# Gated recurrence: the span products of levels 32, 16, 8 and 4 cut into 64 keys by 32 queries, one half of the array's columns for each half tile, and their picks in two parts

## What is computed

```
def hgrn2_chunkwise(q, log_f, k, v):
    ...
    b = jnp.cumsum(lfc, axis=2)
    o_inter = jnp.einsum('bhtk,bhkv->bhtv', qc * jnp.exp(b), state)
    diff = b[:, :, :, None, :] - b[:, :, None, :, :]
    decay = jnp.exp(jnp.where(causal, diff, -jnp.inf))
    attn = jnp.einsum('bhtk,bhsk,bhtsk->bhts', qc, kc, decay)
    o_intra = jnp.einsum('bhts,bhsv->bhtv', attn, vc)
    b_last = b[:, :, -1, :]
    k_dec = kc * jnp.exp(b_last[:, :, None, :] - b)
    new_state = jnp.exp(b_last)[..., None] * state + jnp.einsum('bhsk,bhsv->bhkv', k_dec, vc)
    return new_state, o_inter + o_intra
```

## Time and profile before

| | |
|---|---|
| median of 3 runs | 2033.02 us (2029.32 to 2034.14) |
| profiled execution, its time | 2031.16 us |
| its span | 2029.2 us, 27449 instructions |
| TensorE busy | 1973.9 us, 97% |
| VectorE busy | 1352.0 us, 67% |
| ScalarE, GpSimd busy | 824.5 us, 941.1 us |
| level products (L1164) | 640 records, from 113.3 to 586.9 us |

### The profile page before, as it was taken

The page is one execution under the profiler, slowest core; times in us unless marked ns, Lnnn a source line. Parts: engine busy times, 40 slices in busy tenths (PEclk is TensorE's granted clock), DMA queues, the critical chain, the costliest instruction groups (busy, mean ns, idle before and its releaser), DMA issues.

```text
span 2029.2 us, 27449 instructions
## 1 busy us (share of the span) xinstructions
PE 1973.9 (97%) x10053; PEld 1623.2 (80%) x10053; DVE 1352.0 (67%) x1784; ACT 824.5 (41%) x1313; POOL 941.1 (46%) x548
## 2 busy tenths in 40 slices
PE   7999999999999999999999899898999999999997
PEld 6888888888887768878888678776888888888886
DVE  7887777666536754687061487798856656667978
ACT  5444444344411014463200476657323323334443
POOL 1354454422324459753354110855755455445553
PEclk8999999999999999999999899999999999999999
DMA  9223222211122244044110200222423323357344
GB/s 285 75 81 117 73 72 103 84 40 31 42 63 58 68 156 135 11 177 126 42 51 11 84 2 1 73 104 80 139 88 109 114 88 109 103 183 242 104 137 164
DMA packets 179501, 193.98 MB, mean 96 GB/s; under 512 B 9863, under 2 KB 122968, under 8 KB 179418
## 3 DMA queue, kind: packets, MB, share of 16 engines
q1 hardware_dynamic: 172996, 178.53, 27.8%
q10 hardware_dynamic: 6422, 14.37, 2.0%
HBM read 151.71 MB, written 41.16 MB: 95 GB/s over the span
## 4 chain that ended last, share of the span: by engine, by line
PE 80%; DVE 10%; ACT 5%; issue 3%; POOL 1%; ACTq 0%; DVEq 0%; POOLq 0%
PE psum L1003 7%; PE psum L1558 7%; PE psum L1560 7%; PE psum L1559 7%; PE psum L1005 6%; PE psum L1004 6%; PE psum L1164 3%; PE psum L1661 3%; PE psum L1662 3%; PE psum L1663 3%; PE psum L1024 3%; PE psum L1025 3%; PE psum L1023 3%; PE psum L1319 2%; PE psum L1321 2%
## 5 line engine op out<-in xcount | busy, mean ns | idle before, releaser
L795 POOL TENSOR_TENSOR w_hi<-w_raw,ones 128x1024 fp32r<-128x1024 f32 x60 | 149.2, 2487 | 481.8 <-PE psum L1005 357.5
L1003 PE MATMUL psum<-h_hi,w_hi 128*128 128x512 f32 x704 | 284.2, 404 | 0.0
L1005 PE MATMUL psum<-h_hi,w_lo 128*128 128x512 f32 x704 | 274.8, 390 | 0.0
L1004 PE MATMUL psum<-h_lo,w_hi 128*128 128x512 f32 x704 | 274.2, 389 | 0.0
L798 POOL TENSOR_TENSOR w_lo<-w_raw,w_hi 128x1024 fp32r<-128x1024 f32 x60 | 166.7, 2779 | 4.7
L1693 ACT ACTIVATE arena<-psum 128x1024 f32<-128x1024 f32 (+7 forms) x103 | 80.3, 787 | 216.4 <-PE psum L1005 136.0
L1003 PEld LDWEIGHTS psum<-h_hi,w_hi 128*128 128x128 f32 x704 | 132.3, 188 | 28.5 <-issue 2.6
L1004 PEld LDWEIGHTS psum<-h_lo,w_hi 128*128 128x128 f32 x704 | 132.4, 188 | 28.3 <-issue 2.6
L1005 PEld LDWEIGHTS psum<-h_hi,w_lo 128*128 128x128 f32 x704 | 132.1, 188 | 28.4
L1661 PE MATMUL psum<-w_hi,h_hi 128*128 128x512 f32 x308 | 120.8, 392 | 3.1 <-DVE h_lo L3294 3.1
L993 POOL TENSOR_TENSOR w_lo<-arena,w_hi 128x512 fp32r<-128x512 f32 x61 | 86.3, 1419 | 75.5 <-ACT w_hi L1693 75.5
(11 more groups left out here) (489 smaller groups left out, 5227.5 us busy)
## 6 DMA issues: line engine op xcount, KB each, us to landing
w_raw<-w_in SPq DMA_DIRECT2D x64, 512.0 KB, 3.8
act_op<-arena SPq DMA_DIRECT2D x77, 256.0 KB, 2.3
arena<-act_op SPq DMA_DIRECT2D x77, 256.0 KB, 2.7
w_raw<-w_gate SPq DMA_DIRECT2D x22, 512.0 KB, 4.1
w_raw<-w_up SPq DMA_DIRECT2D x22, 512.0 KB, 5.2
arena<-ada_w SPq DMA_DIRECT2D x16, 512.0 KB, 7.2
arena<-w_out SPq DMA_DIRECT2D x16, 512.0 KB, 5.6
out_T<-arena SPq DMA_DIRECT2D x16, 512.0 KB, 5.8
```

The source lines that it names most:

```text
L1003: pe.matmul(o, wh, xh, start=(k == 0), stop=False)
L1004: pe.matmul(o, wh, xl, start=False, stop=False)
L1005: return pe.matmul(o, wl, xh, start=False, stop=(k == KT - 1))
```

## The change

For the levels 32, 16, 8 and 4 each tile's product is cut in two. The first half takes the tile's first 64 columns as keys and the 32 late columns among them, and writes to PSUM's partitions 0 to 63. The second takes the other 64 and their 32, and writes to partitions 64 to 127. A tile's results fill 32 columns of the bank, not 64, so the level fills 256 of 512. The products of a key in one half of the tile with a query in the other, which no level of 32 or less wants, are no longer made. Level 64, the semaphores and the order of the tasks stay. A pick is two copies of 64 partitions by 256 values, each with its half of the mask, and `pick_done` is given once, by the second.

```
-                    rows = 64 if w == 64 else P
-                    o = psum[0:rows, SPAN_BANK[j], 64 * i:64 * (i + 1)].rearrange("p (n w) -> p n w", w=w)
-                    mm = pe.matmul(o, kq[:, 0:rows], late, start=True, stop=True)
+                    if w == 64:
+                        o = psum[0:64, SPAN_BANK[j], 64 * i:64 * (i + 1)].rearrange("p (n w) -> p n w", w=w)
+                        mm = pe.matmul(o, kq[:, 0:64], late, start=True, stop=True)
+                    else:
+                        nb = 32 // w
+                        for e in range(2):
+                            o = psum[64 * e:64 * e + 64, SPAN_BANK[j], 32 * i:32 * (i + 1)].rearrange("p (n w) -> p n w", w=w)
+                            mm = pe.matmul(o, kq[:, 64 * e:64 * e + 64], late[:, nb * e:nb * (e + 1), :], start=True, stop=True)
...
-                    data = data.rearrange("p (i n w) -> p i n w", i=NT, w=w)
-                    m = m.rearrange("p (a n w) -> p a n w", a=1, w=w).to_broadcast([P, NT, nb, w])
-                    dve.copy_predicated(to, m, data).then_inc(pick_done, 1)
+                    data = data[:, 0:256].rearrange("p (i n w) -> p i n w", i=NT, w=w)
+                    for e in range(2):
+                        rows, blocks = slice(64 * e, 64 * e + 64), slice(nb // 2 * e, nb // 2 * (e + 1))
+                        mask = m[rows, 32 * e:32 * e + 32].rearrange("p (a n w) -> p a n w", a=1, w=w).to_broadcast([64, NT, nb // 2, w])
+                        x = dve.copy_predicated(to[rows, :, blocks, :], mask, data[rows])
+                    x.then_inc(pick_done, 1)
```

## The result

The changed kernel takes 2016.1 us (median of four executions, 2014.99 to 2017.1), the kernel before 2033.6 beside it (2029.32 to 2034.2). The ratio is 0.9921, with a 95% interval of 0.9909 to 0.9933: faster by 0.8%, clear of no change, and 1.9 us under the forecast of 2018. Timed again for the experiments it took 2016.12, ratio 0.9922 (0.9904 to 0.994). The profiled execution took 2014.99 us with a span of 2013.0, where that of before took 2031.16 with 2029.2: 16.2 us less. Later lines moved down with the edit: the level products stand at L1169 (level 64 still at L1164), `task_ms` at L1195, the picks at L2614, `back_3` at L2664.

A forecast was written before the change was run, and what follows sets the result against it. TensorE, busy 97% of the span, was taken as the bound. 28 level tasks x 0.54 = 15.1 us off the profiled 2031.16 gives 2016.1, plus 1.9 for the median: 2018 us; range 2011 to 2031, its own 2013 to 2022.

The forecast's parts named there:

- The task: Each task of levels 32, 16, 8 and 4: 1.47 us against 2.01, entry included, so 0.54 us less.
- the price of the entry: Ahead of a level task's first matmul: entering the half-array form costs 0.09 us more.
- The swallowed gain: At L1140 in four heads: level 4's saving returns as longer waits, 1.6 us each; four tasks lose 2.2 us.
- The picks: VectorE's masked copies in two parts: 0.13 us more a level, 4.1 in all, counted as 0 because VectorE idles there.
- The sum: Whole kernel: 28 x 0.54 = 15.1 us less, 2016.1 profiled; the median 1.9 higher, given as 2018.
- the halves don't load together: Rival, level tasks: a pair of loads costs 0.112 us, each task 0.26 more, kernel 2041 us; 10 in 100.
- A fixed time for each record: Rival, level tasks: each short matmul has a floor, middle 0.044 us; 3.1 us saved, kernel 2030; 9 in 100.
- The gain of the first heads: Rival, heads 0 to 3: chain grows by what levels 32, 16, 8 save; 8.6 us gained, 2024; 10 in 100.
- The opposite case: Heads 0 to 3: L2562 falls clear of L822, four waits go, 4.3 + 2.2 us more, 2011.4; chance 10 in 100.

## Why the prediction was right, step by step

**The task.** 0.54 us was priced, and the trace has 0.53 (0.535 over the tasks). Both of its parts held: the level from its first matmul to L1004 in 1.39 us where 1.38 was said, and the price of the entry, 252.84 - 252.52 = 0.32 where before had 256.19 - 255.96 = 0.23, so 0.09. That loads go in pairs was read from a place that ran in the same form (L1445), and their pitch from level 64, not from the size of the product; that is why it fitted. Within the 1.39 two errors cancel, which is luck. From the first record to the last it is 1.12 - 0.22 = 0.90 us, not 0.93, since the pitch is 0.058 and not 0.062; and from there to L1004 it is 0.49, not 0.45, so the 0.03 that I took off for the shorter last stream is not to be found there.

**The swallowed gain.** The chain was read rightly: in the four heads L1140 is tied to GpSimd's L795 ahead of level 4. From L795 to L1140 it was 296.12 - 270.94 = 25.18 us in the earlier trace rows; in the changed kernel, head 2:

```profile
266.44 2.38 POOL L795 TENSOR_TENSOR w_hi<-w_raw,ones 128x1024 fp32r<-128x1024 f32 x1 [4.69 <-PE psum L1005]
...
272.12 3.34 POOL L822 TENSOR_TENSOR arena<-arena 128x1024 f32<-128x1024 f32 x1
```

```profile
282.10 1.98 PE L1195 MATMUL psum<-arena,ones 128*128 128x512 f32 x4 [0.19 <-ACT arena L1858]
...
291.51 1.06 PE L1140 MATMUL psum<-ident,arena 128*128 128x128 f32 x8 [1.10 <-DVE arena L2664]
```

291.51 - 266.44 = 25.07, the same within 0.1. What failed is the place of the wait. I had put the time at L1140, 1.6 us each, and it stayed at 1.1. The same chain feeds `task_ms` on the way, through ScalarE's squares (L1858), and TensorE is there 9.4 us before L1140. Having saved level 4, it now came too early there and waited first at L1195; what it lost there it could not lose again. The loss is 2.14 - 1.75 = 0.39 us a head and 1.6 us in all, as much as the weight loads there wait longer (2.4 for 0.8). 2.2 was said; the difference is mostly that the chain itself got 0.11 shorter in each of these heads. The row of before could have told: the loads of L1190 waited 0.2 us for the squares already, so there was no slack at that place. A chain that ties the end of a stretch may tie something within it too, and the list of who waits for each link tells that.

VectorE's L2567 ends 0.48 us after L822's end (273.17 + 2.77 against 272.12 + 3.34), as L2562 did by 0.50. The Trainium skill (SBUF — State Buffer, SBUF: two separate sides) says that VectorE, with two operands from SBUF, and GpSimd share a pair of ports that one instruction holds to its end while the other is blocked. The traces agree for L2567: 0.62 us alone against 2.77 here.

**The picks.** 0.424 us was taken, 0.439 measured, and 32 more copies cost VectorE 28.1 - 23.0 = 5.1 us where 4.1 was said. Set at nothing, they cost about 1.8 us alone by the run with only the picks cut. Together with the halved products nothing of it shows: the changed kernel is 1.0 below the one with picks in one piece, within the spread. There level 4 is done 0.54 us sooner after the release of GpSimd's row, and the operation behind the last pick (L2547 now) starts at 392.35, ahead of L798 at 392.89, as before and not as in the run with only the picks cut. So the count of zero held by the place of two operations and not, as I had argued, by the idle time ahead of the picks.

**The sum.** 32 x 0.535 = 17.1, less 1.6: 15.5, where 15.1 stood in the prediction; the loop shows 15.7 and the whole profiled execution 16.2. That is 1.1 of the 1.9 us between 2018 and 2016.1. The other 0.8 is the way from profiled execution to median: 1.9 was carried over from before, and the changed kernel has 1.1.

**The rivals.** That the halves don't load together was wrong for this order and right for the other: 2039.07 against the 2041 it was priced at. What decides is whether records close to each other in the list lie in different halves. A fixed time for each record of the list doesn't exist at this size: 0.0088 us a record in the quarters, under the 0.033 that was the lowest row to be had. By the Trainium skill's 60 cycles for each matmul (TensorEngine Tiling (Array Packing), Instruction Overhead) the 32 matmuls of a quartered task would take an estimated 0.8 us at 2.4 GHz, and 1.6 if each record counted. No such floor for the list as a whole is in the trace: 0.555 us from the first to the last, 42 cycles a matmul. Within one quarter a matmul comes only about every 169 cycles, so whether there is a floor of 60 for each quarter no run here shows. The traces don't agree either with the rule of the Trainium skill (TensorE: Matmul & The Clock Gate, Part 3, the mechanism) that a load overlaps running matmuls only if its row group differs. All of these matmuls use all rows, and in level 16 of head 2 the loads are busy for 1.01 of the 1.12 us in which its matmuls run. The gain of the first heads was not swallowed whole (1.75 of 2.14 came through). The opposite case, L2562 falling clear, didn't come by itself but was made with the sums moved: 6.9 us, where 4.3 + 2.2 was said. The prediction gave it a chance of 10 in 100 in words, but its list of chances adds up to 100 without it.

## What to carry to other kernels

Where small f32 products are bound by weight loads (here 128 columns of weights for 64 moving ones), cut them by blocks of output partitions and let neighbours in the list alternate between halves or quarters of the columns. A pair costs what a single load of its width does (0.058 us for 64 columns), and four of 32 columns came in 0.035; what one of those costs alone was not measured. Leave products whole that can't be cut, but let them alternate too. Read the price from a place of the kernel that already runs in that form, add the 0.09 us of the entry, and look for the chain that ties the stretch to something ahead of it: there the gain ends, and there the next one lies. Look too at which operations of VectorE and GpSimd stand close together: a shift of 0.15 us turned a 1.22 us operation into one of 3.34.

## What the runs showed that I had not expected

- Matmuls of 32 weight columns and 16 moving ones in four quarters run at 0.0088 us a record, four in about 0.035, though one load of that form lasts 0.110 (mean). A load of 64 columns followed by another in the same half comes at 0.058, and so does a pair in two halves. Where a list of eight tiles in one half meets one in the other, eight records ran side by side at 0.028 each.
- 64 such records are through in 0.74 us, and behind them at the loop's end TensorE stood 0.34 us for nothing but its own instructions.
- Picks in two parts, 0.15 us longer each, cost 1.8 us in a kernel whose VectorE idled 57.2 us ahead of them, mostly by putting one VectorE operation behind a GpSimd one in two heads.
- The running sums on VectorE took 4.86 us for eight, and 11.25 under four GpSimd operations in a row. An engine at 69% of the span set the end of those heads.
